# Prompt attention with turns three and values six items behind the scores, and layer norm rows scaled by ScalarE

## Chip, core and metric

One core of a Trainium2 chip runs the whole program. The metric is the device time of one execution in microseconds. Of the kernel before, three runs are shown, and one execution was profiled.

## What is computed

One inference step of a decoder trunk with two layers, for a prompt of 1024 tokens and eight samples of eight tokens each, 1088 rows in all. What matters here are the layer norms and the prompt's attention (cut from the reference):

```python
def _layer_norm(x, g, b, eps=1e-5):
    mu = jnp.mean(xf, -1, keepdims=True)
    var = jnp.mean(jnp.square(xf - mu), -1, keepdims=True)
    return ((xf - mu) * lax.rsqrt(var + eps) * g + b).astype(x.dtype)

# latent attention, 8 heads, blocks of 128 queries, causal
s = (jnp.einsum('bqhl,bsl->bhqs', ql, ckv) + jnp.einsum('bqhr,bsr->bhqs', qr, kr)) * scale
s = jnp.where(k_pos <= qp, s, -jnp.inf)
p = jax.nn.softmax(s, axis=-1)
o = jnp.einsum('bhqs,bsl->bqhl', p, ckv)     # then times w_uv

# a layer
x = _layer_norm(DEEPNORM_ALPHA * x + gate1 * mix, ln1_g, ln1_b)
...
x = _layer_norm(DEEPNORM_ALPHA * x + gate2 * f, ln2_g, ln2_b)
```

A norm of the input rows stands ahead of the first layer, so there are five in a step.

## The kernel before

The program is written engine by engine with semaphores; nothing is reordered by a scheduler. It is a chain of stages, each a block in which the five engines run their own instruction lists, and a barrier of all engines ends each stage (`run`). Ahead of the loop stand the loads, the first modulation vectors and the norm of the input. A loop over the two layers runs the input projection, the recurrent unit, the gated linear attention, the prompt's attention (`stage_mla_prompt`), the samples' attention, the output projection, a norm, the feed-forward part and a norm.

**The layer norm** (`ln_back` with `ln_rows`). The activations lie transposed in `xT`, features across partitions. TensorE transposes a block of 128 rows into two banks of PSUM (L233, eight transposes); four such slots exist, so the block four further waits until this one is scaled. VectorE takes statistics of the block (L250, L251), aggregates them to mean and variance (L252); ScalarE takes the root (L240); one block later VectorE forms the reciprocal (L258) and scales the row, (v - mean) * rstd, into `z` (L259). There are nine blocks, the last of 64 rows. When all nine are done, TensorE transposes `z` back (L286, 72 transposes in 24 groups), and ScalarE and VectorE take turns at multiplying by gain and bias into `xT` (L302, L316). In the norm ahead of the loop the rows come from SBUF and are not transposed first.

**The prompt's attention** (`stage_mla_prompt`). The work is a list of 64 items: head pair (four), query block in the order 7, 0, 6, 1, 5, 2, 4, 3, and the head of the pair. An item of query block q has q + 1 blocks of 128 keys; "seven blocks" below means query block 6. For each item TensorE makes the scores (L1277) and adds the causal mask by a product (L1279), into one of two PSUM slots; VectorE finds the negated maximum (L1480); ScalarE takes exp with the row sum (L1401) into a buffer `probs`; VectorE inverts the sum (L1485); ScalarE scales the probabilities (L1389); TensorE turns them, one transpose a block (L1289); VectorE copies the turned ones into `probsT` (L1493); and for every two items TensorE multiplies them with the values (L1301), which ScalarE copies out (L1383, `keep`). Between the items of one head pair stand the ten projections of the next (L1252 for keys, L1249 for queries, L1256 for the samples' latent queries), one an item from the third on, all into PSUM bank 7: each waits for ScalarE's copy of the one before (L1375, L1373, L1377) and VectorE's part of it (L1462, L1471, L1473). The last head pair has no projections beside it.

The order on each engine is fixed by the loops over `i`. At step i TensorE does the scores of item i, at even i the values of the pair that ended with item i - 3, a projection, and the turn of item i - 2:

```python
for i in range(NI + 4):
    if i < NI:
        scores(i)
    if i >= 4 and i % 2 == 0:
        values(i // 2 - 2)
    for hp, j in pj_at.get(i, []):
        project(hp * NPJ + j)
    if 2 <= i < NI + 2:
        turn(i - 2)
```

ScalarE at step i does the copy of values (odd i), the exp of item i, the scaling of item i - 1 and its copy of a projection; VectorE does the maximum of item i, the reciprocal of item i - 1, its copy of a projection and the copies of item i - 2. There are three buffers `probs` of 1024 columns; the exp of item i waits until item i - 3 is turned.

Of the kernel before, what the change touches and what calls it, by code (L numbers as in the profile page):

```python
# [23 lines left out]
ALU = mybir.AluOpType  # L24
# [98 lines left out]
def build(nc, a, out, n_phys):  # L123
    ctx = ExitStack()
    with ctx:
# [22 lines left out]
        MV = at("mean_var", o, [P, 2, 2]); o += up(32)  # L148
        SD = at("ln_std", o, [P, 2, 1]); o += up(32)
        RS = at("ln_rstd", o, [P, 2, 1]); o += up(32)  # L150
# [71 lines left out]

        def ln_rows(pe, dve, act, src, tr, st, sq, nm, lk):

            if pe is not None:
                for blk in range(NBLK):
                    n = rows(blk)
                    if blk >= 4:  # L230
                        pe.wait_ge(nm, blk - 3)
                    for c in range(KD):
                        ins = pe.transpose(bank(2 * (blk % 4), 2)[0:n, c * P:c * P + P],  # L233
                                           src[:, c, blk * P:blk * P + n], ident)
                    ins.then_inc(tr, 1)
            if act is not None:
                for blk in range(NBLK):
                    n = rows(blk)
                    act.wait_ge(st, blk + 1)
                    act.activation(SD[0:n, blk % 2, :], MV[0:n, blk % 2, 1:2], ACT.Sqrt,  # L240
                                   bias=EPS[0:n, 0:1]).then_inc(sq, 1)
            if dve is not None:
                def stats(blk):
                    n = rows(blk)
                    if src is not None:
                        dve.wait_ge(tr, blk + 1)
                        v = bank(2 * (blk % 4), 2)
                    else:
                        v = Z[:, blk, :]
                    dve.bn_stats(STT[0:n, blk % 2, 0, :], v[0:n, 0:512])  # L250
                    lk(dve.bn_stats(STT[0:n, blk % 2, 1, :], v[0:n, 512:1024]))  # L251
                    dve.bn_aggr(MV[0:n, blk % 2, :], STT[0:n, blk % 2, :, :]).then_inc(st, 1)  # L252

                def norm(blk):
                    n = rows(blk)
                    v = bank(2 * (blk % 4), 2) if src is not None else Z[:, blk, :]
                    dve.wait_ge(sq, blk + 1)
                    lk(dve.reciprocal(RS[0:n, blk % 2, :], SD[0:n, blk % 2, :]))  # L258
                    dve.tensor_scalar(Z[0:n, blk, :], v[0:n, :], MV[0:n, blk % 2, 0:1],  # L259
                                      RS[0:n, blk % 2, :], ALU.subtract, ALU.mult).then_inc(nm, 1)  # L260
                for blk in range(NBLK + 1):
                    if blk < NBLK:
                        stats(blk)
                    if blk:
                        norm(blk - 1)

        def ln_back(g_col, b_col, src, name, modulate=None):


            tr, st, sq, nm = (sem(name + x) for x in ("_rows_in_psum", "_mean_var", "_std", "_row_done"))  # L270
            tb, ea, ed, xd, pj, pm = (sem(name + x) for x in (
                "_back_in_psum", "_back_act", "_back_dve", "_params", "_inbox", "_modulated"))
            gg = [(c, n) for c in range(KD) for n in range(3)]
            with nc.Block() as block:
                @block.tensor
                def _(pe):
                    if src is not None:
                        ln_rows(pe, None, None, src, tr, st, sq, nm, None)
                    pe.wait_ge(nm, NBLK)
# [18 lines left out]
                @block.scalar  # L298
                def _(act):
                    ln_rows(None, None, act, src, tr, st, sq, nm, None)  # L300
                    act.wait_ge(xd, 1)
                    back(act, 0, lambda o, i, s, b: act.activation(o, i, ACT.Identity, bias=b, scale=s))  # L302
                    if modulate is not None:
                        act.wait_ge(ed, len(gg) // 2)
                        act.wait_ge(ea, len(gg) // 2)
                        for c in range(0, KD, 2):
                            modulate_prompt(act, c, *modulate)

                @block.vector
                def _(dve):  # L310
                    lk = chain(dve, name + "_dve")
                    ln_rows(None, dve, None, src, tr, st, sq, nm, lk)
                    dve.tensor_scalar(PRM[:, g_col:g_col + 16], PRM[:, g_col:g_col + 16], ALPHA, None,
# [773 lines left out]
        assert o <= end, (o, end)  # L1087
        PR = at("probs", o_tokb, [P, 3, TP])
        assert 3 * TP * 4 <= r2 - o_tokb
# [13 lines left out]
        def stage_mla_prompt():  # L1103
# [20 lines left out]

            QORD = (7, 0, 6, 1, 5, 2, 4, 3)
            items = [(hp, qb, f) for hp in range(HP) for qb in QORD for f in range(2)]
            NI, PER = len(items), 2 * SMP
# [26 lines left out]
            with nc.Block() as block:  # L1154
# [46 lines left out]
                def _(pe):  # L1201
# [80 lines left out]
                    def turn(i):  # L1282
                        pe.wait_ge(s_pn, i + 1)
                        for t in t_of[i]:
# [3 lines left out]
                            for j in range(n):  # L1288
                                ins = pe.transpose(bank(4 + t % 2)[:, j * P:j * P + P],  # L1289
                                                   PR[:, i % 3, (j0 + j) * P:(j0 + j) * P + P], ident)  # L1290
                            ins.then_inc(s_pt, 1)
# [14 lines left out]
                    for i in range(NPJ):  # L1306
                        project(i)
                    for i in range(NI + 4):
                        if i < NI:
                            scores(i)  # L1310
                        if i >= 4 and i % 2 == 0:
                            values(i // 2 - 2)
                        for hp, j in pj_at.get(i, []):
                            project(hp * NPJ + j)
                        if 2 <= i < NI + 2:
                            turn(i - 2)

# [30 lines left out]
                def _(act):  # L1348
# [37 lines left out]
                    def scale(i):  # L1386
                        act.wait_ge(s_rc, i + 1)
                        v = PR[:, i % 3, 0:scores_item(i)]
                        act.mul(v, v, SUMS[:, i % 4:i % 4 + 1]).then_inc(s_pn, 1)  # L1389
# [4 lines left out]
                    for i in range(NI):  # L1394
                        nk = scores_item(i)
                        if i >= 5 and i % 2:
                            keep((i - 5) // 2)
                        act.wait_ge(s_mx, i + 1)
                        if i >= 3:
                            act.wait_ge(s_pt, t_of[i - 3][-1] + 1)  # L1400
                        act.activation(PR[:, i % 3, 0:nk], bank(2 * (i % 2), 2)[:, 0:nk], ACT.Exp,  # L1401
                                       bias=NM[:, i % 2:i % 2 + 1], accum_out=SUMS[:, i % 4:i % 4 + 1]).then_inc(s_ex, 1)
# [4 lines left out]
                    scale(NI - 1)  # L1407
                    for m in range((NI - 1 - 5) // 2 + 1, NI // 2):
                        keep(m)

                @block.vector
                def _(dve):
# [83 lines left out]
                    for i in range(NPJ):  # L1496
                        read(i)
                    for i in range(NI + 2):
                        if i < NI:
                            maximum(i)  # L1500
                        if 1 <= i <= NI:
                            invert(i - 1)
                        for hp, j in pj_at.get(i, []):
                            read(hp * NPJ + j)
                        if i >= 2:
                            take(i - 2)
                    dve.wait_ge(s_sn, SB)
# [662 lines left out]
```

## Time and profile before

| | us |
|---|---|
| median of 3 runs | 4065.81 (4063.87 to 4066.87) |
| the profiled execution's own time | 4065.0 |
| its span, first to last instruction | 4063.2 |
| TensorE busy (mean granted clock 0.912 of full) | 3520.5 |
| VectorE, ScalarE busy | 1617.6, 1068.2 |
| prompt attention, layer 0, scores to last values | 573.3 to 775.6 |
| prompt attention, layer 1 | 2548.1 to 2750.1 |
| first layer norm in the loop, first statistics to start of the way back | 1181.5 to 1207.6 |
| norm ahead of the loop, first statistics to start of the way back | 58.3 to 79.3 |

PE is TensorE's matmul, DVE is VectorE, ACT is ScalarE, POOL is GpSimd, PEld TensorE's weight load. Times in the timelines are microseconds from the span's start. PEclk is the granted clock as a share of the full 2.4 GHz; at 0.50 it is 1.2 GHz. A busy TensorE is one with a matmul under way. Busy time says nothing of what a change is worth where an engine waits for another, so the stretches and the timelines of the two places are what the prediction reads.

### The profile page before, as it was taken

How to read it: one execution, taken by the hardware profiler on the slowest of the kernel's cores; microseconds unless marked ns; L12 is line 12 of the kernel's file. 1: busy time of each engine (PE TensorE's matmuls, PEld its weight loads, DVE VectorE, ACT ScalarE, POOL GpSimd, SP SyncE). 2: the span in 40 equal slices, each digit the busy share in tenths (PEclk: the TensorE clock that was granted, in tenths of full speed). 3: DMA queues.
4: the chain of work that ended last, by engine and by line, in shares of the span. 5: the costliest groups of instructions: out<-in, count | busy, mean ns of one | idle time of the engine just before them, and what ended most of it. 6: DMA issues, size and time to landing. Idle time of an engine off the chain costs nothing. (4 is left out here: it accounts for less than half of the span.)

```text
span 4063.2 us, 53746 instructions
## 1 busy us (share of the span) xinstructions
PE 3520.5 (87%) x22344; PEld 2996.5 (74%) x22344; DVE 1617.6 (40%) x3034; ACT 1068.2 (26%) x2051; POOL 167.8 (4%) x240
## 2 busy tenths in 40 slices
PE   2985869899888999999969486889999699999997
PEld 1772435566778999999958343566669699999996
DVE  4224556544443222222351445664443523222325
ACT  2122145444313111111131312553431311212112
POOL 0000011111000000000000100201100000000000
PEclk8995779999888999999979667999999799999998
DMA  4112410244101111111111052004421011111111
GB/s 152 39 29 97 156 28 1 85 165 156 53 1 47 43 46 41 48 42 47 32 40 32 27 189 67 1 1 179 164 74 41 27 44 47 44 49 38 51 37 54
DMA packets 80879, 255.64 MB, mean 63 GB/s; under 512 B 15435, under 2 KB 30957, under 8 KB 69494
## 3 DMA queue, kind: packets, MB, share of 16 engines
q1 hardware_dynamic: 68054, 164.04, 12.3%
q0 software_dynamic: 11520, 83.89, 5.8%
q8 instruction: 180, 2.95, 0.3%
q10 hardware_dynamic: 1056, 4.19, 0.3%
q14 instruction: 69, 0.57, 0.0%
HBM read 245.59 MB, written 6.51 MB: 62 GB/s over the span
## 5 line engine op out<-in xcount | busy, mean ns | idle before, releaser
L362 PE MATMUL psum<-h_hi,w_ffn_hi 128*128 128x384 f32 (+1 forms) x2112 | 697.7, 330 | 37.4 <-DVE w_ffn_lo L1955 37.4
L364 PE MATMUL psum<-h_hi,w_ffn_lo 128*128 128x384 f32 (+1 forms) x2112 | 694.6, 329 | 0.0
L363 PE MATMUL psum<-h_lo,w_ffn_hi 128*128 128x384 f32 (+1 forms) x2112 | 684.9, 324 | 0.0
L362 PEld LDWEIGHTS psum<-h_hi,w_ffn_hi 128*128 128x128 f32 x2112 | 397.6, 188 | 37.7 <-DVE w_ffn_lo L1955 37.7
L363 PEld LDWEIGHTS psum<-h_lo,w_ffn_hi 128*128 128x128 f32 x2112 | 397.7, 188 | 0.0
L364 PEld LDWEIGHTS psum<-h_hi,w_ffn_lo 128*128 128x128 f32 x2112 | 396.6, 188 | 0.0
L364 PE MATMUL psum<-ffn_act_hi,w_ffn_lo 128*128 128x384 f32 (+1 forms) x1056 | 344.7, 326 | 0.0
L363 PE MATMUL psum<-ffn_act_lo,w_ffn_hi 128*128 128x384 f32 (+1 forms) x1056 | 344.4, 326 | 0.0
L362 PE MATMUL psum<-ffn_act_hi,w_ffn_hi 128*128 128x384 f32 (+1 forms) x1056 | 344.1, 326 | 0.0
L348 DVE SCALAR_TENSOR_TENSOR xT<-psum,adaT,xT 128x384 f32<-128x384 f32 (+1 forms) x240 | 136.6, 573 | 419.6 <-PE psum L364 419.6
L1971 DVE TENSOR_TENSOR ffn_act<-silu_tmp,psum 128x384 f32<-128x384 f32 x132 | 70.3, 532 | 562.8 <-PE psum L364 562.8
L1955 DVE TENSOR_TENSOR w_ffn_lo<-w_ffn,w_ffn_hi 128x1024 fp32r<-128x1024 f32 (+2 forms) x152 | 164.7, 1085 | 294.2 <-ACT w_ffn_hi L1930 294.2
L1930 ACT CAST w_ffn_hi<-w_ffn 128x1024 fp32r<-128x1024 f32 (+2 forms) x152 | 141.9, 935 | 405.0 <-DMA w_ffn<-in_w_down 313.8
L362 PEld LDWEIGHTS psum<-ffn_act_hi,w_ffn_hi 128*128 128x128 f32 x1056 | 198.2, 188 | 0.0
L364 PEld LDWEIGHTS psum<-ffn_act_hi,w_ffn_lo 128*128 128x128 f32 x1056 | 198.2, 188 | 0.0
L363 PEld LDWEIGHTS psum<-ffn_act_lo,w_ffn_hi 128*128 128x128 f32 x1056 | 198.2, 188 | 0.0
L1942 ACT CAST ffn_act_hi<-ffn_act 128x384 fp32r<-128x384 f32 x132 | 65.5, 497 | 442.5 <-DVE ffn_act L1971 442.5
L1939 ACT ACTIVATE silu_tmp<-psum 128x384 f32<-128x384 f32 x132 | 62.7, 475 | 433.6 <-PE psum L364 433.6
L1277 PE MATMUL psum<-kT,qT 96*128 96x512 f32 (+3 forms) x384 | 154.5, 513 | 13.2 <-POOL qT L1189 12.6
L1693 ACT COPY keysT<-psum 128x512 f32<-128x512 f32 x192 | 106.9, 590 | 201.2 <-PE psum L1603 201.2
L1603 PEld LDWEIGHTS psum<-consts,pages 128*128 128x128 f32 x1024 | 112.6, 144 | 53.4 <-issue 51.0
L1747 DVE TENSOR_REDUCE dec_max<-psum 128x1 f32<-128x1024 f32 x64 | 78.4, 1225 | 169.3 <-PE psum L1619 169.3
(363 smaller groups left out, 5932.9 us busy)
## 6 DMA issues: line engine op xcount, KB each, us to landing
w_ada_pair<-in_w_ada SPq DMA_DIRECT2D x48, 1024.0 KB, 5.0
w_ffn<-in_w_gu SPq DMA_DIRECT2D x88, 512.0 KB, 3.5
w_ffn<-in_w_down SPq DMA_DIRECT2D x32, 384.0 KB, 3.1
w_ffn<-in_w_down SPq DMA_DIRECT2D x32, 320.0 KB, 2.9
w_out<-in_w_out SPq DMA_DIRECT2D x16, 512.0 KB, 7.0
w_in_T<-in_w_in_T SPq DMA_DIRECT2D x12, 512.0 KB, 4.3
z<-in_x_prompt SPq DMA_DIRECT2D x1, 4096.0 KB
w_ada_first<-in_w_ada SPq DMA_DIRECT2D x2, 2048.0 KB, 17.1
```

The lines of the kernel that those rows point to most:

```text
L348: ins = eng.scalar_tensor_tensor(XT[:, c, t0:t0 + wp], ps[:, 0:wp], ADA[:, gate + c, 0:1], XT[:, c, t0:t0 + wp], ALU.mult, ALU.add)
L362: pe.matmul(o, wh, xh, start=first, stop=False)
L363: pe.matmul(o, wh, xl, start=False, stop=False)
L364: return pe.matmul(o, wl, xh, start=False, stop=last)
L1277: ins = pe.matmul(o_[:, 0:w], q, KT[:, s, 512 * b:512 * b + w], start=True, stop=not last)
L1603: ins = pe.transpose(bank(n % 3)[:, j * P:j * P + P], src, ident)
L1693: copy(dst, src).then_inc(done, 1)
L1747: lk(dve.tensor_reduce(MXD[:, s % 2, :], bank(3, 2), AX.X, ALU.max))
L1930: act.copy(WHI[:, i % NSW, 0:nk].bitcast(F32R), WRAW[:, i % NSW, 0:nk]).then_inc(s_wh, 1)
L1942: act.copy(UH[:, f - f0, t0:t0 + w].bitcast(F32R), UT[:, f - f0, t0:t0 + w]).then_inc(s_uh, 1)
L1955: dve.tensor_tensor(WLO[:, i % NSW, 0:nk].bitcast(F32R), WRAW[:, i % NSW, 0:nk], WHI[:, i % NSW, 0:nk], ALU.subtract).then_inc(s_wl, 1)
L1971: dve.tensor_tensor(UT[:, c - f0, t0:t0 + w], SGT[:, n, 0:w], bank(g % 8)[:, 0:w], ALU.mult).then_inc(s_um, 1)
```

## The change

In the attention there are four probability buffers: two of 1024 columns for query blocks 7 to 4 and two of 512 for 0 to 3, in the place of three of 1024. The exp of item i waits for the turn of item i - 4. At step i TensorE now does the scores of item i, the turn of item i - 3, a projection, and at even i the values of the pair that ended with item i - 5. VectorE copies item i - 3, ahead of its part of a projection. ScalarE's copy of values moves by two items.

In the norm VectorE forms the reciprocal and, with one small operation, -mean * rstd; ScalarE scales the row as Identity(v * rstd + bias), one step behind its root. VectorE's reciprocal also waits until the row of two blocks earlier is scaled, whose two numbers it overwrites.

```diff
-        SD = at("ln_std", o, [P, 2, 1]); o += up(32)
+        SD = at("ln_std", o, [P, 2, 2]); o += up(32)
...
             if act is not None:
+                def norm(blk):
+                    n = rows(blk)
+                    v = bank(2 * (blk % 4), 2) if src is not None else Z[:, blk, :]
+                    act.wait_ge(rs, blk + 1)
+                    act.activation(Z[0:n, blk, :], v[0:n, :], ACT.Identity, bias=SD[0:n, blk % 2, 1:2],
+                                   scale=RS[0:n, blk % 2, :]).then_inc(nm, 1)
                 for blk in range(NBLK):
                     n = rows(blk)
                     act.wait_ge(st, blk + 1)
-                    act.activation(SD[0:n, blk % 2, :], MV[0:n, blk % 2, 1:2], ACT.Sqrt,
+                    act.activation(SD[0:n, blk % 2, 0:1], MV[0:n, blk % 2, 1:2], ACT.Sqrt,
                                    bias=EPS[0:n, 0:1]).then_inc(sq, 1)
+                    if blk:
+                        norm(blk - 1)
+                norm(NBLK - 1)
...
                 def norm(blk):
                     n = rows(blk)
-                    v = bank(2 * (blk % 4), 2) if src is not None else Z[:, blk, :]
                     dve.wait_ge(sq, blk + 1)
-                    lk(dve.reciprocal(RS[0:n, blk % 2, :], SD[0:n, blk % 2, :]))
-                    dve.tensor_scalar(Z[0:n, blk, :], v[0:n, :], MV[0:n, blk % 2, 0:1],
-                                      RS[0:n, blk % 2, :], ALU.subtract, ALU.mult).then_inc(nm, 1)
+                    if blk >= 2:
+                        dve.wait_ge(nm, blk - 1)
+                    lk(dve.reciprocal(RS[0:n, blk % 2, :], SD[0:n, blk % 2, 0:1]))
+                    dve.scalar_tensor_tensor(SD[0:n, blk % 2, 1:2], MV[0:n, blk % 2, 0:1], -1.0, RS[0:n, blk % 2, :],
+                                             ALU.mult, ALU.mult).then_inc(rs, 1)
...
-        PR = at("probs", o_tokb, [P, 3, TP])
+        PRL = at("probs_long", o_tokb, [P, 2, TP])
+        PRS = at("probs_short", o_tokb + 2 * TP * 4, [P, 2, TP // 2])
...
+            def probs(i):
+                return (PRS if i // 2 % 2 else PRL)[:, i % 2]
...
-                    for i in range(NI + 4):
+                    for i in range(NI + 6):
                         if i < NI:
                             scores(i)
-                        if i >= 4 and i % 2 == 0:
-                            values(i // 2 - 2)
+                        if 3 <= i < NI + 3:
+                            turn(i - 3)
                         for hp, j in pj_at.get(i, []):
                             project(hp * NPJ + j)
-                        if 2 <= i < NI + 2:
-                            turn(i - 2)
+                        if i >= 6 and i % 2 == 0:
+                            values(i // 2 - 3)
...
-                        if i >= 5 and i % 2:
-                            keep((i - 5) // 2)
+                        if i >= 7 and i % 2:
+                            keep((i - 7) // 2)
                         act.wait_ge(s_mx, i + 1)
-                        if i >= 3:
-                            act.wait_ge(s_pt, t_of[i - 3][-1] + 1)
-                        act.activation(PR[:, i % 3, 0:nk], bank(2 * (i % 2), 2)[:, 0:nk], ACT.Exp,
+                        if i >= 4:
+                            act.wait_ge(s_pt, t_of[i - 4][-1] + 1)
+                        act.activation(probs(i)[:, 0:nk], bank(2 * (i % 2), 2)[:, 0:nk], ACT.Exp,
...
-                    for i in range(NI + 2):
+                    for i in range(NI + 3):
                         if i < NI:
                             maximum(i)
                         if 1 <= i <= NI:
                             invert(i - 1)
+                        if i >= 3:
+                            take(i - 3)
                         for hp, j in pj_at.get(i, []):
                             read(hp * NPJ + j)
-                        if i >= 2:
-                            take(i - 2)
```

The change's lines are numbered 14 higher in the attention and some 8 to 10 higher in the norm. TensorE in the first head pair, from the scores of item 5 to the work behind item 6, before (L1277 and L1279 are scores and mask, L1249 a projection, L1289 a turn, L1301 values; in the change L1291, L1293, L1263, L1303 and L1315):

```order
L1277 MATMUL psum<-kT,qT 128x512
L1277 MATMUL psum<-kT,qT 128x384
L1279 MATMUL psum<-causal_bf,ident_bf 128x128
L1249 MATMUL psum<-q_normT,w_uq 128x384 x2
L1289 MATMUL psum<-consts,probs 128x128
L1277 MATMUL psum<-kT,qT 128x256
L1279 MATMUL psum<-causal_bf,ident_bf 128x128
L1301 MATMUL psum<-probsT,v 64x128 x2
L1249 MATMUL psum<-q_normT,w_uq 128x320 x2
L1289 MATMUL psum<-consts,probs 128x128 x7
```

And in the change:

```order
L1291 MATMUL psum<-kT,qT 128x512
L1291 MATMUL psum<-kT,qT 128x384
L1293 MATMUL psum<-causal_bf,ident_bf 128x128
L1303 MATMUL psum<-consts,probs_short 128x128
L1263 MATMUL psum<-q_normT,w_uq 128x384 x2
L1291 MATMUL psum<-kT,qT 128x256
L1293 MATMUL psum<-causal_bf,ident_bf 128x128
L1303 MATMUL psum<-consts,probs_short 128x128
L1263 MATMUL psum<-q_normT,w_uq 128x320 x2
L1315 MATMUL psum<-probsT,v 64x128 x16
```

The turn moved ahead of the projection and is that of an item earlier; the values moved behind the projection and are those of the pair before. Between two projections there are now the scores and a turn, but no values at odd steps.

VectorE in the first layer norm of the loop, from the reciprocal of block 0 to the aggregate of block 2, before:

```order
L258 RECIPROCAL ln_rstd<-ln_std 128x1
L259 TENSOR_SCALAR z<-psum,mean_var,ln_rstd 128x1024
L250 BN_STATS stats<-psum 128x6
L251 BN_STATS stats<-psum 128x6
L252 BN_AGGR mean_var<-stats 128x2
```

And in the change:

```order
L268 RECIPROCAL ln_rstd<-ln_std 128x1
L269 SCALAR_TENSOR_TENSOR ln_std<-mean_var,ln_rstd 128x1
L259 BN_STATS stats<-psum 128x6
L260 BN_STATS stats<-psum 128x6
L261 BN_AGGR mean_var<-stats 128x2
```

The operation on 1024 columns has left VectorE, and one on a single column stands in its place. On ScalarE the scaling (L241 of the change) stands behind the root of the next block (L246); no table load stands between them.

## Rows read from the trace of the kernel before

**Rows 1.** the page, part 1: busy time, share of the span, instructions:

```profile
PE 3520.5 (87%) x22344; PEld 2996.5 (74%) x22344; DVE 1617.6 (40%) x3034; ACT 1068.2 (26%) x2051; POOL 167.8 (4%) x240
```

**Rows 2.** stretches: length, busy per engine, PEclk, DMA share, GB/s:

```profile
573.30:627.30 54.00, 50.45 (x268) 30.96 (x269) 31.03 (x64) 27.50 (x61) 8.38 (x18) 0.84 0.00 1
677.10:727.00 49.90, 45.84 (x315) 29.85 (x314) 33.35 (x71) 28.42 (x66) 7.52 (x14) 1.00 0.00 1
727.00:775.60 48.60, 40.74 (x327) 28.09 (x326) 27.60 (x63) 26.99 (x61) 0.00 (x0) 0.96 0.01 1
```

**Rows 3.** stretches, inside the last head pair of layer 0:

```profile
740.00:750.00 10.00, 7.80 (x60) 5.52 (x59) 4.50 (x10) 5.11 (x11) 0.00 (x0) 0.87 0.00 0
```

**Rows 4.** timeline, TensorE, third pair: start, us, instruction, [idle before, releaser]:

```profile
684.66 1.09 PE L1301 MATMUL psum<-probsT,v 128*64 128x128 f32 x16 [1.25 <-DVE probsT L1493]
688.14 1.13 PE L1252 MATMUL psum<-ckvT,w_uk 128*128 128x512 f32 x2 [0.17 <-ACT kT L1375]
699.65 0.44 PE L1301 MATMUL psum<-probsT,v 128*64 128x128 f32 x4 [0.94 <-DVE probsT L1493]
700.36 1.34 PE L1249 MATMUL psum<-q_normT,w_uq 128*128 128x320 f32 x4 [0.27 <-ACT qT L1373]
```

**Rows 5.** timeline, first layer norm in the loop: VectorE, then TensorE:

```profile
1186.08 0.69 DVE L250 BATCH_NORM_STATS2 stats<-psum 128x6 f32<-128x512 f32 x1
1187.67 1.34 DVE L259 TENSOR_SCALAR z<-psum,mean_var,ln_rstd 128x1024 f32<-128x1024 f32 x1
1188.93 0.69 DVE L250 BATCH_NORM_STATS2 stats<-psum 128x6 f32<-128x512 f32 x1
1186.22 1.09 PE L233 MATMUL psum<-consts,xT 128*128 128x128 f32 x8 [0.66 <-DVE z L259]
1191.92 1.97 PE L233 MATMUL psum<-consts,xT 128*128 128x128 f32 x8 [1.76 <-DVE z L259]
```

**Rows 6.** groups of instructions: count, busy us, mean ns, idle before:

```profile
L2066 ACT ACTIVATE z<-psum 128x1024 f32<-128x1024 f32 (+1 forms) x9 | 8.6, 1030 | 5.2 <-PE psum L2057 5.2
L329 ACT ACTIVATE hT<-xT,adaT 128x1024 f32<-128x1024 f32 x20 | 23.2, 1229 | 2.0 <-DVE xT L316 2.0
L240 ACT ACTIVATE ln_std<-mean_var,eps 128x1 f32<-128x1 f32 (+1 forms) x45 | 13.2, 294 | 98.6 <-DVE mean_var L252 98.6
L1485 DVE RECIPROCAL mla_sums<-mla_sums 128x1 f32<-128x1 f32 x128 | 20.1, 157 | 7.0 <-ACT probs L1401 5.8
```

**Rows 7.** timeline, VectorE, layer norm ahead of the loop:

```profile
63.64 0.81 DVE L259 TENSOR_SCALAR z<-z,mean_var,ln_rstd 128x1024 f32<-128x1024 f32 x1
64.37 0.69 DVE L250 BATCH_NORM_STATS2 stats<-z 128x6 f32<-128x512 f32 x1
65.96 0.81 DVE L259 TENSOR_SCALAR z<-z,mean_var,ln_rstd 128x1024 f32<-128x1024 f32 x1
```

**Rows 8.** timeline, item 5 of the third pair: TensorE, then ScalarE:

```profile
696.54 0.22 PE L1279 MATMUL psum<-causal_bf,ident_bf 128*128 128x128 bf16 x1
697.92 1.01 ACT L1401 ACTIVATE probs<-psum,mla_neg_max 128x896 f32<-128x896 f32 x1 [2.17 <-DVE mla_neg_max L1480]
699.85 0.46 ACT L1373 COPY qT<-psum 64x384 f32<-64x384 f32 x1
```

**Rows 9.** timeline, items 1 and 9 of the third pair: TensorE and ScalarE:

```profile
682.47 0.22 PE L1279 MATMUL psum<-causal_bf,ident_bf 128*128 128x128 bf16 x1
687.51 0.57 ACT L1375 COPY kT<-psum 64x512 f32<-64x512 f32 x1
711.44 0.22 PE L1279 MATMUL psum<-causal_bf,ident_bf 128*128 128x128 bf16 x1
714.41 0.41 ACT L1373 COPY qT<-psum 64x320 f32<-64x320 f32 x1
```

**Rows 10.** stretches, the same layer norm:

```profile
1200.00:1208.00 8.00, 0.41 (x2) 0.41 (x3) 7.44 (x14) 0.59 (x2) 0.00 (x0) 0.50 0.00 0
1208.00:1215.00 7.00, 7.00 (x42) 5.69 (x41) 3.87 (x6) 4.00 (x7) 0.00 (x0) 0.74 0.00 0
```

More of the change, by code:

```diff
@@ L220, in bc, with ln_rows @@
             return ap.unsqueeze(len(ap.shape)).to_broadcast(list(ap.shape) + [n])
-        def ln_rows(pe, dve, act, src, tr, st, sq, nm, lk):
+        def ln_rows(pe, dve, act, src, tr, st, sq, rs, nm, lk):
             if pe is not None:
@@ L267, in ln_back @@
         def ln_back(g_col, b_col, src, name, modulate=None):
-            tr, st, sq, nm = (sem(name + x) for x in ("_rows_in_psum", "_mean_var", "_std", "_row_done"))
+            tr, st, sq, rs, nm = (sem(name + x) for x in ("_rows_in_psum", "_mean_var", "_std", "_rstd", "_row_done"))
             tb, ea, ed, xd, pj, pm = (sem(name + x) for x in (
@@ L277, in _ @@
                     if src is not None:
-                        ln_rows(pe, None, None, src, tr, st, sq, nm, None)
+                        ln_rows(pe, None, None, src, tr, st, sq, rs, nm, None)
                     pe.wait_ge(nm, NBLK)
@@ L299, in _ @@
                 def _(act):
-                    ln_rows(None, None, act, src, tr, st, sq, nm, None)
+                    ln_rows(None, None, act, src, tr, st, sq, rs, nm, None)
                     act.wait_ge(xd, 1)
@@ L311, in _ @@
                     lk = chain(dve, name + "_dve")
-                    ln_rows(None, dve, None, src, tr, st, sq, nm, lk)
+                    ln_rows(None, dve, None, src, tr, st, sq, rs, nm, lk)
                     dve.tensor_scalar(PRM[:, g_col:g_col + 16], PRM[:, g_col:g_col + 16], ALPHA, None,
@@ L1289, in turn @@
                                 ins = pe.transpose(bank(4 + t % 2)[:, j * P:j * P + P],
-                                                   PR[:, i % 3, (j0 + j) * P:(j0 + j) * P + P], ident)
+                                                   probs(i)[:, (j0 + j) * P:(j0 + j) * P + P], ident)
                             ins.then_inc(s_pt, 1)
@@ L1387, in scale @@
                         act.wait_ge(s_rc, i + 1)
-                        v = PR[:, i % 3, 0:scores_item(i)]
+                        v = probs(i)[:, 0:scores_item(i)]
                         act.mul(v, v, SUMS[:, i % 4:i % 4 + 1]).then_inc(s_pn, 1)
@@ L1407, in _ @@
                     scale(NI - 1)
-                    for m in range((NI - 1 - 5) // 2 + 1, NI // 2):
+                    for m in range((NI - 1 - 7) // 2 + 1, NI // 2):
                         keep(m)
```

## Prediction

> **What bounds the kernel now.** I read the page first: one span, and TensorE busy 87% of it [rows 1]. So only time in which TensorE waits can be won, or time in which it runs below full clock. The change touches two places; for each I went to the stretches, then to the timelines of TensorE, VectorE and ScalarE.
>
> Prompt attention takes 202 us in each of the two layers: four head pairs of 16 items. The table of stretches [rows 2] gives TensorE's busy time in the first, third and last pair; the second is like the third. The third pair lasts 49.90 us with 45.84 busy: 4.06 us of waits. The last pair has no projections to put between: 48.60 with 40.74 busy, 7.86 us of waits. There TensorE also falls to the lower clock once: a mean of 0.87 over 10 us [rows 3] is 2.6 us at half clock, about 1.3 us lost. The timeline of TensorE [rows 4] shows who it waits for: the value products wait for VectorE's copy of the turned probabilities (1.25 and 0.94 us), a projection for ScalarE's copy of the one before it (0.17 and 0.27). A turn is asked for right behind the scores of two items later, and the values right behind that.
>
> In the layer norm of rows, VectorE sets the pace and everything else waits: one block's statistics start at 1186.08, its neighbour's scaling at 1187.67, the next statistics at 1188.93 [rows 5]. So 2.85 us a block: 1.59 of statistics, aggregate and reciprocal, 1.26 of scaling. There are five such norms, nine blocks each.
>
> **The norm: scaling goes to ScalarE.** VectorE loses the 1.26 and gains one operation on 128x1 numbers. The trace has no such operation; a reciprocal of as many takes 0.157 us [rows 6]. I take 0.15, between 0.05 (wholly overlapped) and 0.3. A block then costs VectorE 1.59 + 0.15 = 1.74, or 1.11 less. ScalarE's new work: from PSUM 1.030 us for 128x1024 with constants, and 1.229 for the same size with scale and bias as columns [rows 6]; I take 1.23, plus the square root of 0.294 that it has now [rows 6]: about 1.5, below 1.74, so VectorE still sets the pace. The scaled rows come out one step later, but today's tail (reciprocal, scaling, reciprocal, scaling, 2 x 1.26 and small pieces) and the new one (two scalings of 1.2 on ScalarE behind the last reciprocals) are within 0.2 us of each other. Between the first reciprocal and the eighth lie seven blocks: 7 x 1.11 = 7.8 us.
>
> TensorE feeds the blocks. Blocks 4 to 8 wait for the scaling of four blocks earlier; at the lower clock eight transposes take 1.97 us [rows 5], more than 1.74. Five blocks at 0.23 are 1.2 us at worst; since the first of them run at 1.09 today, I take 0.3. That leaves 7.5 us for each of the four norms from PSUM: **30 us**. The new waits cost nothing: VectorE's wait for the scaling of two blocks before is over a block old when it is met, and the square root stands ahead of the scaling in ScalarE's queue.
>
> The first norm reads its rows in SBUF. There VectorE scales in 0.73 (63.64 to 64.37) of a block of 2.32 (63.64 to 65.96) [rows 7]. The gain is 0.73 - 0.15 = 0.58 a block, 4.1 in seven; the tail is longer by about 1, as two scalings of 1.2 follow where two of 0.8 stood. **3 us.**
>
> Here the trace contradicts a caution. In PSUM VectorE takes 1.34 for the scaling [rows 5], ScalarE 1.03 to 1.23 [rows 6]; in SBUF VectorE's 0.81 is the quicker [rows 7]. The Trainium skill, ScalarE: Activation LUTs, section Rules for kernel authors, says that multiplies and adds belong on VectorE, up to about three times as fast per element in bf16. Taken at that factor on 0.81, the first norm would have ScalarE at 2.4 + 0.29 a block and lose 3 us instead of winning 3, and the whole would come to about 4018; the fp32 rows here speak against the factor.
>
> **Attention: turns three items behind, values six.** No matrix work is added; 64 items' scores, turns and values stay. A fourth probability buffer lets ScalarE's exp wait for the turn of four items earlier. That turn is queued on TensorE behind the scores of the item before, ahead of this item's scores, so this wait is never the last. A turn now uses rows scaled a whole step earlier, and the values use copies three steps old: the waits of 1.25 and 0.94 and their like go. What is late next is the projection. All of a later pair's projections use one PSUM bank, so each needs ScalarE's copy of the one before, and that copy stands in ScalarE's queue behind this item's exp and the scaling of the item before. This chain is not shortened, while the values that TensorE did ahead of it now come behind it. Three places of a pair show it:
>
> - Item 5 (seven blocks): from its mask matmul at 696.54, exp at 697.92, copy 699.85 + 0.46 [rows 8]: the next projection may start 3.82 later, as it does today at 700.36 [rows 4]. Of these 3.82 TensorE today idles 1.21 and spends 0.44 on values; the turn that moves in adds 0.11. It will wait 3.82 - 2.28 = 1.5 (1.21 today).
> - Item 9: 711.44 to the copy's end at 714.82 is 3.4 [rows 9]; TensorE has item 5's 2.28 with scores of three blocks for two (0.2 more), turns of two for one (0.2) and a narrower projection (0.24 less): 2.45. It waits 1.0.
> - Second key projection: 682.47 to 688.08 (copy 687.51 + 0.57) is 5.6 [rows 9]; of the 5.67 up to 688.14 TensorE today idles 1.25 + 0.17 [rows 4], leaving 4.25; values one block longer (0.2) and one more turn of four blocks (0.45) make 4.9. It waits 0.8.
>
> That is 3.3 us of waits where 4.06 stand: 0.75 saved in a pair with projections, 2.2 in three. The first pair loses nothing more: its start is at the lower clock, mean 0.84 [rows 2], where TensorE is slow against the others.
>
> The last pair has no projections. What stays by the same adding up is 0.8 at the turn of its first item and 0.6 in the drain, where two more turns and one more pair of values fill the end. 7.86 + 1.3 - 1.4 = 7.8. A layer saves 10, two layers **20 us**. The bounds: nothing in the pairs with projections (16), or all waits gone but the drain's (some 40).
>
> **Sum.** 30 + 3 + 20 = 53 us. The profiled execution took 4065.0, the median of the runs is 4065.8, so they stand for each other: 4065 - 53 = **4012**. Each stage ends at a barrier of all engines, so a stage's gain goes to the end whole.
>
> **Rivals.**
>
> 1. TensorE keeps its clock in the norms. From 1200 to 1208, ahead of the transposes back, it is busy for 0.41 us and the granted clock is 0.50; the first 7 us of them then run at 0.74 [rows 10], 3.6 us at half clock, 1.8 lost. If closer row transposes and a pause of 4 us instead of 8 keep it up, five norms give 9 and the four row phases 1 more: 4002. For it: the same transposes take 1.09 right after a busy stage [rows 5]. Against: the pause stays, and TensorE is at most 63% busy (1.09 of 1.74). The Trainium skill, TensorE: Matmul & The Clock Gate, Part 1, says the throttled state is the default and activity lifts it, which is what these rows show. Chance 0.15.
> 2. ScalarE sets the norms' pace. If a scaling from PSUM with both columns costs 1.43 (1.23 and once more the 0.20 between the two rows [rows 6]), with the square root's 0.29 and a handover of 0.35 from VectorE (reciprocal and small operation) that is not hidden, a block takes 2.07: 0.33 x 40 blocks = 13 us less: 4025. Chance 0.08.
> 3. The change does not do in attention what it says: the waits move from turns and values to the projections one for one, and only the norms win: 4032. For it: 3.3 of 4.06 come back by my own count. Against: the last pair has no projections. Chance 0.10.
> 4. Slower. ScalarE falls a step behind, and every projection waits for an exp and a scaling that it does not wait for now, 1.93 us at seven blocks (697.92 to 699.85 [rows 8]). 60 projections at 1.93 instead of the 0.33 counted are 96 us: 4108. It decides from a mean wait of 0.33 + 53/60 = 1.2 us a projection. Against: ScalarE is busy 28.42 of 49.90 us [rows 2], and the copies of small items are early. Chance 0.05, of it 0.03 slower and 0.02 about even.
>
> **How the numbers follow.** The forecast has 0.62. Its own bounds (0.3 instead of 0.15 on VectorE: 6 us; the row transposes: 4; the projections' waits: 6 either way) give 4002 to 4022. With rivals 1 and 2, and half of 3, 0.8 and more lies in 3995 to 4031. A change of 0.2%, 8 us, is about what a measurement of this kernel can tell from none. All cases but the fourth are faster by more than that: 0.95; the same 0.02, slower 0.03.
>
> **What would show it.** Right: VectorE's blocks in the norms 1.7 to 1.8 us apart, ScalarE's scaling 1.1 to 1.25, the transposes back starting 7 to 8 us sooner; in attention TensorE no longer waiting at value products, a wait of 1 to 1.6 us at the projections behind items 5 and 9, the last pair near 41 us, the others near 49. Wrong: scalings over 1.5 us, row transposes as the norm's pace, waits at turns, or a last pair above 45.

## Result and the profile after

The changed kernel takes 4006.43 us (median of four runs, 3996.53 to 4010.72) beside 4066.34 for the kernel before: a ratio of 0.9846, 95% interval 0.9823 to 0.9869, or 60 us less. The forecast was 4012, in a range of 3995 to 4031. The same kernel, timed twice more, had 4006.99 and 4006.95. The profiled execution is the shortest of its four: 3996.53, span 3994.4.

Busy time by engine; it answers to [rows 1]. VectorE has 55 us less and ScalarE 54 more: the norms' scaling. TensorE has the same 22344 instructions, in 33 us less busy time: it ran more of them at the higher clock (mean granted clock 0.924, before 0.912).

```profile
PE 3487.3 (87%) x22344; PEld 2975.3 (74%) x22344; DVE 1563.1 (39%) x3034; ACT 1122.4 (28%) x2096; POOL 168.7 (4%) x240
```

The four head pairs of layer 0 in the table of stretches, columns as in [rows 2]:

```profile
565.80:616.35 50.55, 47.50 (x252) 29.04 (x253) 29.69 (x62) 27.38 (x60) 8.36 (x18) 0.86 0.00 1
616.35:665.35 49.00, 45.67 (x314) 29.76 (x313) 32.54 (x71) 28.68 (x66) 7.52 (x14) 1.00 0.00 1
665.35:714.36 49.01, 45.68 (x315) 29.78 (x313) 32.55 (x71) 28.68 (x66) 7.52 (x14) 1.00 0.01 1
714.36:757.00 42.64, 40.57 (x346) 28.29 (x344) 27.94 (x65) 27.08 (x62) 0.00 (x0) 1.00 0.01 2
```

The pairs in the middle take 49.0 where 49.8 stood, and TensorE still idles 49.01 - 45.68 = 3.3 us in each. The last fell from 48.6 to 42.6, the first from 54.0 to 50.6. Over both layers, the value products waited 27.4 us for VectorE's copies; now that wait is gone. The two groups, before and after, with the idle time ahead of them:

```profile
L1301 PE MATMUL psum<-probsT,v 128*64 128x128 f32 x1152 | 77.0, 278 | 27.4 <-DVE probsT L1493 27.4
L1315 PE MATMUL psum<-probsT,v 128*64 128x128 f32 x1152 | 77.0, 278 | 0.9 <-ACT hT L1397 0.9
```

The timeline of TensorE in the third pair shows where the 3.3 us are. These three rows answer to [rows 4]; three projections wait now:

```profile
676.08 1.12 PE L1266 MATMUL psum<-ckvT,w_uk 128*128 128x512 f32 x2 [0.77 <-ACT kT L1389]
687.33 1.34 PE L1263 MATMUL psum<-q_normT,w_uq 128*128 128x320 f32 x4 [1.59 <-ACT qT L1387]
701.86 0.43 PE L1270 MATMUL psum<-qT,w_ukT 64*128 64x64 f32 x2 [0.97 <-ACT qT L1387]
```

The first norm in the loop, as in [rows 5]: two blocks' statistics on VectorE and what lies between; the root and the scaling on ScalarE; then TensorE's row transposes and the way back, the transposes of `z`; its last row is that of the kernel before.

```profile
1164.95 0.69 DVE L259 BATCH_NORM_STATS2 stats<-psum 128x6 f32<-128x512 f32 x1
1166.41 0.11 DVE L268 RECIPROCAL ln_rstd<-ln_std 128x1 f32<-128x1 f32 x1
1166.55 0.16 DVE L269 SCALAR_TENSOR_TENSOR ln_std<-mean_var,ln_rstd 128x1 f32<-128x1 f32 x1
1166.63 0.69 DVE L259 BATCH_NORM_STATS2 stats<-psum 128x6 f32<-128x512 f32 x1
```

```profile
1166.52 0.30 ACT L246 ACTIVATE ln_std<-mean_var,eps 128x1 f32<-128x1 f32 x1 [0.24 <-DVE mean_var L261]
1166.74 1.21 ACT L241 ACTIVATE z<-psum,ln_std,ln_rstd 128x1024 f32<-128x1024 f32 x1
```

```profile
1166.33 1.09 PE L233 MATMUL psum<-consts,xT 128*128 128x128 f32 x8 [1.14 <-ACT z L241]
1173.05 1.06 PE L233 MATMUL psum<-consts,xT 128*64 128x128 f32 x8 [0.59 <-ACT z L241]
1179.15 13.59 PE L296 MATMUL psum<-consts,z 128*128 128x128 f32 x72 [5.05 <-ACT z L241]
1207.59 11.73 PE L286 MATMUL psum<-consts,z 128*128 128x128 f32 x72 [8.06 <-DVE z L259]
```

A block takes 1166.63 - 1164.95 = 1.68 us where it took 2.85. The new operation on 128x1 numbers costs 0.16, the scaling on ScalarE 1.21. ScalarE waits for VectorE in every block, 0.24 here, so VectorE sets the pace. The pause ahead of the way back fell from 8.06 to 5.05, but the way back itself took 13.59 instead of 11.73.

| from the timelines, us | before | after |
|---|---|---|
| four norms from PSUM, first row transpose to start of the way back | 27.38, 27.79, 26.89, 26.89 | 19.30, 18.39, 18.38, 19.50 |
| their ways back | 11.73, 11.34, 13.73, 11.55 | 13.59, 13.70, 11.40, 11.85 |
| both, summed | 157.3 | 126.1 |
| first norm, first statistics to way back | 20.94 | 17.26 |
| attention's scores to the next stage's first transpose, by layer | 216.8, 215.6 | 205.5, 204.1 |
| gated linear attention, first to last sum of its forget gates (code untouched), by layer | 123.4, 123.5 | 118.4, 118.2 |

So the profiled span, 68.8 us shorter, consists of 31.2 in the four norms, 22.8 in attention, 10.3 in a stage that the change doesn't touch, and some 4 at the start and between.

### The profile page after: what moved, and what is told of

Same layout as the page of the kernel before. It is cut to its first block and busy times, and to the rows that moved or that the text cites. A ratio compares the mean times of both kernels' runs of the same rounds, so it can differ in the third digit from the quotient of the medians.

```text
span 3994.4 us, 53828 instructions
## 1 busy us (share of the span) xinstructions
PE 3487.3 (87%) x22344; PEld 2975.3 (74%) x22344; DVE 1563.1 (39%) x3034; ACT 1122.4 (28%) x2096; POOL 168.7 (4%) x240
## 5 line engine op out<-in xcount | busy, mean ns | idle before, releaser
L1291 PE MATMUL psum<-kT,qT 96*128 96x512 f32 (+3 forms) x384 | 157.9, 521 | 15.8 <-POOL qT L1203 12.6
L1617 PEld LDWEIGHTS psum<-consts,pages 128*128 128x128 f32 x1024 | 112.7, 143 | 53.5 <-issue 51.0
```

Source lines behind the costliest of these rows:

```text
L1291: ins = pe.matmul(o_[:, 0:w], q, KT[:, s, 512 * b:512 * b + w], start=True, stop=not last)
L1617: ins = pe.transpose(bank(n % 3)[:, j * P:j * P + P], src, ident)
```

## Experiments

The theory is the prediction's: the norm and attention gain in their own stages and add. Two things had to be explained: the 10 us in the untouched stage, and the projections' new waits. Each kernel but the first two is the changed one, unedited, with one edit or with two; times are medians of 4 to 11 runs.

**One part alone.** The two halves of the change, each in the kernel before (`norm_only` has the norm's lines of the diff, `att_only` those of the attention), and the changed kernel once more.

```diff
 norm_only: the lines of stage_mla_prompt stay as before
-            def probs(i):
-                return (PRS if i // 2 % 2 else PRL)[:, i % 2]
...
 att_only: the lines of ln_rows stay as before
-                    act.activation(Z[0:n, blk, :], v[0:n, :], ACT.Identity, bias=SD[0:n, blk % 2, 1:2],
-                                   scale=RS[0:n, blk % 2, :]).then_inc(nm, 1)
...
```

> The kernel before with the norm's part of the change alone. Theory (the parts add): each of the four norms from PSUM has its pause ahead of the transposes back shortened by 8.1 to 8.5 us, the first by 3; minus some 2 where the transposes back run longer at the lower clock: 33 us less, about 4033 (ratio 0.992), VectorE's blocks 1.67 apart. Rival: the 5 us per layer that the gated linear attention stage lost in the profile after (121.6 to 116.6 in the first layer, code untouched) belong to the norm's earlier end: 43 us less, 4023 (0.9895).

> The kernel before with attention's part alone. Theory (the parts add): 11.2 us less in each layer, 22 in all: about 4044 (ratio 0.9945), pairs of 50.5, 49.0, 49.0 and 42.6 us, gated linear attention as long as before. Rival: the waits move one for one, the gain in the profile after came from the norms and the clock: 4065 (1.0). Second rival: the shorter gated linear attention stage belongs to this part: 4034 (0.992).

> The changed kernel once more, unedited, as the reference for the others. Theory: about 4007 (0.9855), and the gated linear attention stages (116.6 us in the first profile) are 5 us longer or shorter from execution to execution, with the granted clock there, so that this profile need not show 116.6. Rival: they are part of the change: 116 to 117 us again and 3997 (0.983).

Measured: `norm_only` 4023.67 (ratio 0.9895, 0.9877 to 0.9913), `att_only` 4040.03 (0.9933, 0.9919 to 0.9948), the changed kernel 4006.99 (0.9851, 0.9836 to 0.9867), before 4065.35. The first is the rival's number, but not by the rival's mechanism. The table of stretches, gated linear attention of layer 0 in the kernel before, in the changed one at its first profile and at a later one (`after_third` below), and in `norm_only`; under the last, two head pairs of its attention:

```profile
362.60:486.00 123.40, 104.75 (x725) 57.26 (x726) 58.79 (x158) 16.65 (x64) 0.00 (x0) 0.71 0.54 188
```

```profile
359.60:478.00 118.40, 99.62 (x725) 54.52 (x726) 58.74 (x158) 16.81 (x64) 0.00 (x0) 0.75 0.56 196
358.60:482.20 123.60, 104.87 (x726) 57.30 (x726) 58.81 (x158) 16.65 (x64) 0.00 (x0) 0.71 0.53 187
```

```profile
357.00:480.20 123.20, 104.52 (x725) 56.82 (x726) 58.80 (x158) 16.65 (x64) 0.00 (x0) 0.71 0.53 188
567.30:617.80 50.50, 46.95 (x258) 28.68 (x259) 29.79 (x61) 26.20 (x58) 8.36 (x18) 0.87 0.00 1
717.40:766.70 49.30, 41.37 (x340) 28.09 (x339) 28.72 (x65) 28.28 (x66) 0.00 (x0) 1.00 0.00 1
```

With the norm's part alone the stage takes 123.2 at a clock of 0.71, as before. The same changed kernel gave 118.4 in one profile and 123.6 in another. In the twelve profiles of this section, two layers each, it lies at 116.9 to 118.9 or at 122.9 to 123.6, in four of them at one in the one layer and at the other in the other. The 10 us belong to one execution and its clock, not to the change; without them the 68.8 are 58.5, about what the medians give.

The four norms gave 31.1 (157.3 to 126.2), as in the whole change. But `norm_only` gained 42 us by its medians where 33 were expected, and 44.6 by the two spans. Of the 10 us beyond the norms (31.1, and 3.7 in the first) half lies in its attention, which with the code of before took 213.6 and 213.6 for 216.8 and 215.6. The first pair of layer 0 rose to full clock earlier (50.5 us at 0.87 for 54.0 at 0.84), and the last pair stayed at it (1.00 for 0.96 [rows 2]). Whether this belongs to the execution or to the norm's part, one profile of each kernel doesn't show; the other half is spread over the stages between. `att_only` gave 216.8 to 205.0 and 215.6 to 204.9: 11.8 + 10.7 = 22.5. The two medians add to 42 + 25 = 67 where the whole gave 58; with intervals of about 7 us on either side that does not contradict adding, and stage by stage the parts do add: 31.1 and 22.5 apart, 31.2 and 22.8 together.

**Distances.** Which part of attention's change ends the waits? First the values back at their old distance; then the turns back at their old place and distance, with the values left at six and again ahead of the projection; then three buffers, where exp again waits for the turn of three items earlier. The lines that follow from these on other engines are left out (...).

```diff
 turn3_values4
-                        if i >= 6 and i % 2 == 0:
-                            values(i // 2 - 3)
+                        if i >= 4 and i % 2 == 0:
+                            values(i // 2 - 2)
...
 values_only
-                        if 3 <= i < NI + 3:
-                            turn(i - 3)
+                        if i >= 6 and i % 2 == 0:
+                            values(i // 2 - 3)
                         for hp, j in pj_at.get(i, []):
                             project(hp * NPJ + j)
-                        if i >= 6 and i % 2 == 0:
-                            values(i // 2 - 3)
+                        if 2 <= i < NI + 2:
+                            turn(i - 2)
...
 three_buffers
-                return (PRS if i // 2 % 2 else PRL)[:, i % 2]
+                return PR[:, i % 3]
...
```

> The changed kernel with the values four items behind the scores (their distance before), turns still three behind, values still last of a step. Theory (the values' distance ended their waits for VectorE's copy): the values now follow right behind the turn that they need, unless a projection stands between, and wait some 1.0 us for the copy; four of eight steps of a pair with projections and all eight of the last: about 4.8 + 4.8 + 4.8 + 8 us a layer, 44 in all, 4050 (0.996). Rival: the turn's distance and the new order within a step are what counts: 4007.

> The changed kernel with turns two items behind and the order in a step as before the change; the values alone stay six items behind. Theory (the values' distance ended the large waits; the turn's move only ends the turns' waits for ScalarE's scaling, 8.5 us in all before, most of it in the last pairs): pairs with projections near 49.0, where the projections' chain decides, the last pair 2.5 to 3 us longer than 40.9: 5 or 6 us in all, about 4012 (0.987). Rival: without the values' waits the turns come to their scalings early and wait for them in every step: 0.5 to 1 us an item, 64 items, two layers: 4060 and more.

> The changed kernel with three probability buffers of full length, as before the change; exp then waits for the turn of three items earlier, which stands behind this item's own scores. Theory: the turn ends ahead of VectorE's maximum for long items, and 0.5 to 0.7 us behind it for the short ones (a maximum of 128 columns takes 0.28, a turn of eight blocks 1.09); the projections behind them wait that much more: 1 to 2 us a pair, 8 to 14 in all, about 4017 (0.988). Rival: TensorE has other work in that time and nothing changes: 4007; the fourth buffer is then not part of the gain.

Measured: `turn3_values4` 4065.45 (1.0011, 1.0002 to 1.0020), no faster than before. The norms keep what they won (123.8 in four); attention takes 231.1 and 235.9, 57 us more than in the changed kernel and 35 more than before. `values_only` 4002.53 (0.9844, 0.9825 to 0.9863), beside the changed kernel at 4006.95 (0.9858) on the same chip. `three_buffers` 4006.63 (0.9869, 0.9854 to 0.9884). Pairs of layer 0, from the mask of one first item to the next, and the last to its final value:

| us | first | second | third | last |
|---|---|---|---|---|
| before | 52.2 | 49.8 | 49.8 | 47.0 |
| `norm_only` (attention as before) | 50.4 | 49.8 | 49.8 | 45.6 |
| changed kernel (`after_third`) | 48.5 | 49.0 | 49.0 | 40.9 |
| `turn3_values4` | 51.4 | 54.1 | 54.1 | 53.5 |
| `values_only` | 46.9 | 46.9 | 46.9 | 43.1 |
| `three_buffers` | 48.6 | 49.0 | 49.0 | 40.9 |
| `copy_first` (below) | 47.0 | 46.6 | 46.6 | 40.9 |
| `values_ahead` (below) | 45.9 | 46.3 | 46.3 | 40.9 |

Groups of TensorE's instructions with the idle time before them: the values in `turn3_values4`, then three groups of `values_only`:

```profile
L1315 PE MATMUL psum<-probsT,v 128*64 128x128 f32 x1152 | 77.2, 279 | 57.1 <-DVE probsT L1507 56.7
```

```profile
L1315 PE MATMUL psum<-probsT,v 128*64 128x128 f32 x1152 | 77.0, 278 | 0.9 <-ACT hT L1397 0.9
L1263 PE MATMUL psum<-q_normT,w_uq 128*128 128x384 f32 (+1 forms) x192 | 68.6, 489 | 0.0
L1303 PE MATMUL psum<-consts,probs_long 128*128 128x128 f32 x416 | 59.5, 282 | 6.8 <-ACT probs_long L1403 6.4 <-DVE probsT L1507 0.3
```

The values' distance is what ended their waits: with the values alone moved, as in `values_only`, they wait no more. At four items they cost 56.7 us, more than the 27.4 of before, because they now stand right behind the turn of the same step, where the next item's scores stood between (expected: 44, at 1.0 a wait; where no projection stands between, a wait is 0.87 to 2.19 in the second and last pair of layer 0). In `values_only` the turns keep a wait for the scaling (6.4 in the row shown), and the last pair is about 2 longer. But its middle pairs are 2.1 shorter than in the changed kernel and its first is 1.6 shorter, and the query projections wait 0.0. That I had not expected: I had put those pairs at 49.0. So part of the change, the turn's new place or the values' place behind the projection, costs more than the turn's distance wins. `values_ahead` below tells which: it keeps the turn's new place and distance and puts the values ahead of the projection, and its pairs are shorter than those of `values_only` by 1.0, 0.6, 0.6 and about 2 us. So the turn's part of the change wins that, and the values' place is what costs. The fourth buffer is no part of the gain. The group of the exps in `three_buffers` shows a wait for turns, 15.8 us over both layers, that the changed kernel does not have, and no pair gets longer by it:

```profile
L1414 ACT ACTIVATE probs<-psum,mla_neg_max 128x128 f32<-128x128 f32 (+7 forms) x128 | 94.6, 739 | 121.6 <-DVE mla_neg_max L1493 105.5 <-PE psum L1302 15.8
```

**The projections' waits.** Two edits, each on one supposed cause: ScalarE's copy stands behind a scaling in its queue; TensorE's values stand behind the projection instead of ahead of it.

```diff
 copy_first
-                        if i:
-                            scale(i - 1)
                         for hp, j in pj_at.get(i, []):
                             read(hp * NPJ + j)
+                        if i:
+                            scale(i - 1)
 values_ahead
+                        if i >= 6 and i % 2 == 0:
+                            values(i // 2 - 3)
                         for hp, j in pj_at.get(i, []):
                             project(hp * NPJ + j)
-                        if i >= 6 and i % 2 == 0:
-                            values(i // 2 - 3)
```

> The changed kernel with ScalarE's copy of a projection ahead of its scaling of the item before. Theory (the projections wait for ScalarE's queue: exp, scaling, copy): the copy comes 0.4 to 1.1 us sooner; the three waits of a pair (1.59, 0.97, 0.77) fall to about 0.7, 0.35 and 0, where VectorE's rotation products (ended 0.9 to 0.05 us ahead of ScalarE's copy) end last: 2.3 us a pair, 14 in six pairs: about 3993 (0.982). Rival: VectorE's read of the same bank or the turn that now waits for a later scaling takes it back: no change, 4007.

> The changed kernel with the values ahead of the projection within a step, as they stood before the change; all distances kept. Theory (the projections wait because the values that used to fill their chain stand behind them): at the even steps the values (1.97 and 1.75 us of work) cover the waits of 1.59 and 0.97, the one of 0.77 at an odd step stays: pairs with projections near 46.5 for 49.0, the last 40.9 as it is; 15 us less than the changed kernel, about 3992 (0.982). Rival: the projection itself then ends later and the next one waits for its copy instead: no change, 49.0 and 4007.

Measured: `copy_first` 3997.16 (0.9828, 0.9810 to 0.9846), `values_ahead` 3991.88 (0.9809, 0.9792 to 0.9826). The pairs are in the table: 2.4 and 2.7 us less in each of the middle ones. The groups show which projections still wait; first the three of the changed kernel, then of `copy_first`, then of `values_ahead`:

```profile
L1263 PE MATMUL psum<-q_normT,w_uq 128*128 128x384 f32 (+1 forms) x192 | 65.6, 472 | 9.4 <-ACT qT L1387 9.4
L1266 PE MATMUL psum<-ckvT,w_uk 128*128 128x512 f32 x32 | 18.4, 669 | 5.5 <-ACT kT L1389 3.8 <-issue 1.7
L1270 PE MATMUL psum<-qT,w_ukT 64*128 64x64 f32 x32 | 6.9, 294 | 6.3 <-ACT qT L1387 6.1 <-ACT q_latT L1391 0.2
```

```profile
L1263 PE MATMUL psum<-q_normT,w_uq 128*128 128x384 f32 (+1 forms) x192 | 65.4, 472 | 4.7 <-DVE rope_tmp L1487 4.7
L1266 PE MATMUL psum<-ckvT,w_uk 128*128 128x512 f32 x32 | 19.4, 701 | 1.7 <-issue 1.7
L1270 PE MATMUL psum<-qT,w_ukT 64*128 64x64 f32 x32 | 6.7, 289 | 2.9 <-ACT qT L1387 2.4 <-ACT q_latT L1391 0.5
```

```profile
L1263 PE MATMUL psum<-q_normT,w_uq 128*128 128x384 f32 (+1 forms) x192 | 67.0, 480 | 0.0
L1266 PE MATMUL psum<-ckvT,w_uk 128*128 128x512 f32 x32 | 20.3, 730 | 4.7 <-ACT kT L1389 3.0 <-issue 1.7
L1270 PE MATMUL psum<-qT,w_ukT 64*128 64x64 f32 x32 | 6.9, 294 | 0.5 <-ACT q_latT L1391 0.5
```

Both causes are real. With the copy ahead of the scaling the wait is left to the other reader of the bank, VectorE's rotation products, as expected. With the values ahead, the projection's chain (exp, scaling, copy) is as long as before, and TensorE has work in it; only the wait at the odd step stays (3.0 at the key projection). The order within a step had given back 2.7 us in each middle pair and 1.9 to 2.6 in the first, 15 us by the medians (4006.95 to 3991.88, on two chips), of what the distances won. `copy_first` has attention at 199.3 and 199.4 for 205.4 and 205.7: 12 of the 14 us expected. `copy_first` and `values_ahead` together were not tried.

**The pause ahead of the way back.** If the lower clock there comes of the pause, work in the pause should keep it up. `warm` lets TensorE make 28 transposes that nobody reads, in PSUM that is free by then.

```diff
+                    if src is not None:
+                        pe.wait_ge(nm, 6)
+                        for r in range(28):
+                            pe.transpose(bank(2)[:, 0:P], src[:, r % KD, 0:P], ident)
                     pe.wait_ge(nm, NBLK)
```

> The changed kernel with 28 transposes that nobody reads, put on TensorE in each of the four pauses ahead of the transposes back. Theory (the pause lets the granted clock fall to 0.50, and the first half of the 72 transposes back runs there): with TensorE kept busy through the pause they run at 1.00 throughout, 9.3 us (28 in 3.70 us at 1.00) where 12.4 to 13.7 stand: 3 to 4 us a norm, 14 in four, about 3993 (0.982). Rival: the added transposes run at the lower clock themselves, end after the last rows are scaled and delay the way back by up to 2.5 us a norm: 4007 to 4017.

> Both edits together: ScalarE's copy of a projection ahead of the scaling (10 us less by itself), and the transposes in the pauses. Theory (they lie in different stages and add): 10 + 14 off 4007, about 3983 (0.980). Rival: the second does nothing, 3997.

> The changed kernel unedited, as the reference of this call. About 4005 (0.9853); pairs of 48.2 to 48.9, 49.0, 49.0 and 40.9 us in both layers.

> ScalarE's copy ahead of the scaling and the transposes in the pauses, beside the changed kernel on one chip. Theory, from the stages measured so far: attention 12 us less (pairs of 46.6 for 49.0, three in each of two layers, with the first less by 1.5), the four norms 10 less (way back 9.88 for 12.5): 22 to 24 less than the changed kernel, about 3982. Rival: nothing beyond the 10 us of the first edit, 3995.

Measured: `warm` 3997.67 (0.9844, 0.9831 to 0.9858); `copy_first_warm` 3982.12 (0.9807, 0.9794 to 0.9821). On that chip the kernel before had 4061.48, so `warm` beside the changed kernel on another chip is unclear by its median; on the same chip it is 9 us below `three_buffers`, which was as long as the changed kernel. Its stretches are clear: the pause with the added transposes, then the way back, at 1.00 throughout, and for comparison the changed kernel's first way back, cut where its clock rose:

```profile
1181.10:1185.66 4.56, 3.28 (x29) 3.04 (x29) 2.43 (x12) 4.04 (x6) 0.00 (x0) 1.00 0.00 0
1185.66:1195.54 9.88, 9.88 (x72) 7.95 (x72) 7.25 (x11) 7.55 (x12) 0.00 (x0) 1.00 0.01 2
```

```profile
1179.15:1187.00 7.85, 7.84 (x33) 6.50 (x34) 2.96 (x5) 3.25 (x5) 0.00 (x0) 0.50 0.00 0
1187.00:1192.74 5.74, 5.74 (x41) 4.42 (x39) 4.28 (x7) 4.31 (x7) 0.00 (x0) 0.96 0.01 3
```

All four ways back take 9.88 or 9.89 us where 11.4 to 13.7 stood, and the four norms 115.3 in sum where the changed kernel has 125.2 to 126.1. On one chip, `both_edits` (the same kernel as `copy_first_warm`) took 3980.53 (0.9793, 0.9774 to 0.9811) beside 4006.95 for the changed kernel: 26 us less, and 83 less than before. Between their two profiles attention has 11.7 less, the norms 11.6, and the stage with two lengths, by its clock, 6. It is the fastest kernel of this study.

## Why the prediction was right, point by point

**Norms, 30 us: 31.** In the first profile 157.3 became 126.1. VectorE's block was put at 1.74 and is 1.68; ScalarE's scaling was put at 1.23 and is 1.21; the small operation was put at 0.15 and is 0.16. Two smaller things were off and nearly cancel. A block saves 2.85 - 1.68 = 1.17 and not 1.11; and the row transposes were to cost 0.3 us, but all that wait for a scaling now run at 1.06 to 1.09 (before in part at 1.97 [rows 5]). So the way to the first transpose back shortens by 8.35 on average, not 7.5. Against that, the ways back grew by 2.2 in sum. So rival 1 was half right: the clock stays up among the rows, but is lost again in the pause of 5 us. Only the filled pauses gave about the 9 us that it had counted on (125.2 to 126.1 down to 115.3). The Trainium skill, TensorE: Matmul & The Clock Gate, Part 1, says that the throttled state is the default and activity lifts it; `warm` agrees: 1.00 with work in the pause, 0.50 at first without.

**First norm, 3 us: 3.7** (20.94 to 17.26). ScalarE's scaling from SBUF takes 1.24 where VectorE's took 0.81 [rows 7], a factor of 1.5 and not the three that the prediction weighed; the first norm won all the same, since VectorE's time is what counts.

**Attention, 20 us: 16 to 23.** The waits at item 5, item 9 and the second key projection were put at 1.5, 1.0 and 0.8; they are 1.59, 0.97 and 0.77, and a pair in the middle saves 0.82 for 0.75. The wrong terms were the first pair, put at 0.75 like the others, and the last. The first takes 48.5 where attention as before takes 50.4 to 52.2. The last saves 6.1 for the forecast 7.8: it takes 42.6 by the bounds of [rows 2], not 41. Its waits are 42.64 - 40.57 = 2.1 us and not 1.4, and TensorE's busy time there stays near 40.6 although the dip of [rows 3] is gone. Part of both misses is work, by the program's order: at the larger distances one more turn and one more pair of values leave the first pair and run at the end. So the two misses have one source in part, and in the sum they cancel. Part is clock: `norm_only`, with attention's code as before, is some 3 us shorter in layer 0 (216.8 to 213.6), with an earlier rise and without the dip. Against `norm_only` a layer saves 8 to 9, against the profile before 11, so that the forecast of 10 lies between by luck in part.

**Rivals.** ScalarE as the norm's pace: no, it idles 0.24 or so in each block. Waits one for one: in the middle pairs nearly so (3.3 of 4.06 us are back, now at projections), in the first and last not. Slower: the price it feared, a projection behind exp and scaling, was there, 19 us in all (9.4 + 6.1 + 3.8, where some 3 stood before) and not 96.

## What to carry to other kernels

When a loop's stages are put further apart, look first at which queue the next wait ends in, and keep the work that fills a chain ahead of the instruction that waits for it: the same values cost 15 us or nothing depending on which side of the projection they stand. Move the elementwise step of a norm to the engine that idles, even if that engine is the slower one at it, as long as its block stays below the pace of the other. And where TensorE pauses a few microseconds ahead of a burst, filling the pause is worth a look: here some 10 us in four places.

## What was not expected of the hardware

The clock's rise comes at very different times in the same work. TensorE was busy for 7.84 of the 7.85 us in which the way back of the first norm stayed at 0.50; in the third norm of the same profile the whole way back took 11.40 for 13.59. Gated linear attention, with the same code in all kernels, had two lengths, about 118 and 123 us, in the same kernel, with mean clocks of 0.75 and 0.71. Differences under some 10 us between two profiles of this program therefore have to be read stage by stage.
